# Keeping the retrieval dots' token rows in PSUM all the time, in a fused encoder layer on one core

## The reference

```python
# attention branch (8 heads, query/key width 96, value width 64), for each block of 128 queries
s = qn @ k_nope + qr @ k_rope
p = softmax(s); o = p @ v
# channel sublayer: retrieval over 16384 experts, 8 heads, top 16 each: 128 experts for every token
u = take(w_u, expert)                    # one row of 1024 values for each token and expert
h = einsum('cd,ced->ce', x, u)           # the "dots"
a = gelu(h) * gate
y = einsum('ce,ced->cd', a, take(w_v, expert))
```

## Time and profile before

| | |
|---|---|
| median of 3 runs | 3766.79 us (3752.15 to 3831.59) |
| the profiled execution | 3753.76 us, its span 3752.0 us |
| first dot, first slot of the loop of group 0 | 510 us, 688 us |
| DMA | 1225 MB, of which 1074 MB gathers |

### The profile page before, as it was taken

The page is one execution under the profiler, slowest core; times in us unless marked ns, Lnnn a source line. Parts: engine busy times, 40 slices in busy tenths (PEclk is TensorE's granted clock), DMA queues, the critical chain, the costliest instruction groups (busy, mean ns, idle before and its releaser), DMA issues.

```text
span 3752.0 us, 40793 instructions
## 1 busy us (share of the span) xinstructions
PE 2602.4 (69%) x13952; PEld 2128.5 (57%) x13952; DVE 2224.7 (59%) x5048; ACT 1618.5 (43%) x1846; POOL 2169.2 (58%) x2075
## 2 busy tenths in 40 slices
PE   6998966587886765777886666767976754544455
PEld 3456655465765664566765655657856644444444
DVE  5233166786655666776666666766566575565542
ACT  1121024455554444555554444555554444344344
POOL 3000035577687566677676556676775566666664
PEclk9999987787998886888998887888988876667667
DMA  4203469899999999999999999999999999999997
GB/s 173 93 29 105 146 257 344 298 352 346 400 409 407 359 362 346 345 349 375 409 409 383 356 346 337 347 342 386 409 409 366 347 341 352 354 337 351 339 351 294
DMA packets 341858, 1225.09 MB, mean 327 GB/s; under 512 B 37841, under 2 KB 45522, under 8 KB 341138
## 3 DMA queue, kind: packets, MB, share of 16 engines
q0 software_dynamic: 294912, 1073.87, 76.2%
q1 hardware_dynamic: 34226, 118.98, 8.5%
q10 hardware_dynamic: 12512, 29.63, 2.1%
HBM read 1206.61 MB, written 15.73 MB: 326 GB/s over the span
## 4 chain that ended last, share of the span: by engine, by line
PE 35%; another core or an unknown queue 21%; ACT 14%; issue 12%; POOL 7%; DMA 5%; DVE 4%; DVEq 1%; ACTq 0%; SPq 0%
PE acc L647 16%; ACT av L1174 10%; POOL rows L347 4%; POOL rows L338 4%; DMA rows<-in_peer_v,ids_peer 3%; PE fA L566 3%; PE mB L612 3%; PE fA L524 2%; PE fB L578 2%; PE mB L542 1%; PE mB L406 1%; DVE rows L946 1%; PE fB L376 1%; DMA rows<-in_peer_u,ids_peer 1%
## 5 line engine op out<-in xcount | busy, mean ns | idle before, releaser
L647 PE MATMUL acc<-ident,av 128*128 128x128 f32 x8192 | 1314.2, 320 | 1019.2 <-ACT av L1174 602.0
L647 PEld LDWEIGHTS acc<-ident,av 128*128 128x128 f32 x8192 | 1140.1, 167 | 1205.8 <-ACT av L1174 687.4
L1174 ACT ACTIVATE av<-rows,coef 128x1024 f32<-128x1024 f32 x1024 | 1155.9, 1145 | 1354.8 <-remote 709.5
L338 POOL DMA_INDIRECT rows<-in_peer_u,ids_peer x1024 | 1070.4, 1045 | 722.6 <-DVE ids_peer L926 309.4
L347 POOL DMA_INDIRECT rows<-in_peer_v,ids_peer x1024 | 1050.7, 1026 | 696.1 <-ACT av L1174 404.7
L946 DVE CUSTOM_DVE_ANT_0 rows<-rows,fB 128x1024 f32<-128x1024 f32 x538 | 647.8, 1216 | 360.6 <-DMA rows<-in_peer_u,ids_peer 322.9
L946 DVE CUSTOM_DVE_ANT_0 rows<-rows,hh 128x1024 f32<-128x1024 f32 x486 | 584.0, 1221 | 157.4 <-DMA rows<-in_peer_u,ids_peer 118.4
L612 PE MATMUL mB<-hT_g,wring 128*128 128x256 f32 x1024 | 246.5, 396 | 1.1 <-ACT hT_g L1136 1.1
L566 PE MATMUL fA<-hT_g,wring 128*128 128x256 f32 x1024 | 241.9, 391 | 3.6 <-issue 3.6
L612 PEld LDWEIGHTS mB<-hT_g,wring 128*128 128x128 f32 x1024 | 202.8, 204 | 28.6 <-ACT hT_g L1136 1.5
L566 PEld LDWEIGHTS fA<-hT_g,wring 128*128 128x128 f32 x1024 | 198.1, 198 | 33.9 <-issue 7.2
(11 more groups left out here) (170 smaller groups left out, 2233.1 us busy)
## 6 DMA issues: line engine op xcount, KB each, us to landing
wring<-in_wstream SPq DMA_DIRECT2D x192, 512.0 KB
rows<-in_peer_u,ids_peer POOLq DMA_INDIRECT x1024
rows<-in_peer_v,ids_peer POOLq DMA_INDIRECT x1024
hT_g<-in_x SPq DMA_DIRECT2D x8, 512.0 KB, 3.6
hres_spill<-KT ACTq DMA_DIRECT2D x8, 512.0 KB, 2.6
hT_spill<-rows ACTq DMA_DIRECT2D x1, 4096.0 KB
wring<-in_wstream SPq DMA_DIRECT2D x16, 256.0 KB
hh<-hres_spill ACTq DMA_DIRECT2D x4, 1024.0 KB
```

The lines of the kernel that those rows point to most:

```text
L338: pool.indirect_dma_start(u_rows[:, ring(g, i, NU), :], None, peer_u, bass.IndirectOffsetOnAxis(ap=ids_peer[:, t, s:s + 1], axis=0)).then_ ...
L647: last = mm(acc[:, tok(k)], av[:, i % NAV, tok(k)], ident[:, :], is_transpose=True, start=i % SLOTS == 0 and k % 4 == 0, stop=i % SLOTS == ...
L1174: s.activation(av[:, i % NAV, :], v_rows[:, ring(g, i, NV), :], ACT.Copy, scale=coef[:, b, i % BATCH:i % BATCH + 1]).then_inc(scaled, 1)
```

## The change

All dots read h1 from fB. For that, fB is freed of the front in every group after the first:

- In groups 1 to 3, the probabilities are turned in two halves through m1: four transposes (step a+7), a DVE copy of 512 columns (a+8), four transposes (a+9), a second copy (a+10). Group 0 still turns all eight through fB.
- The product with V of each head goes to 64 columns of m0 (`pv_at`), the bank that the queries use. So PE must wait with it until the queries of two heads later have been evicted, and with queries until the output of an earlier head has been read. Group 0 uses 64 columns of m1.
- DVE divides the output of each head by itself (a reciprocal of one column and a multiplication of 64 columns), where it did eight heads in one go.
- The turned output is copied in two halves.
- Gates, output projection and layer norm use m0 and m1 in the place of fB's halves (`front_banks`). PE's first such matmul waits until DVE has read the previous group's result out of mB (`y_read`), a wait that stood in front of the K stage before.
- Attention now ends at step 90, so M, O, L and K start ten steps later (M0 = 95, O0 = 143, L0 = 159, K0 = 171), with the lists moved accordingly, and LEAD goes from 40 to 32. Gates start after the last head's output is turned, where they started before it.

```diff
-LEAD = 40
+LEAD = 32
...
-M0, M_PERIOD = 85, 6
-O0 = 133
-L0 = 149
-K0, K_PERIOD = 161, 4
-
-PS0 = 162
+M0, M_PERIOD = 95, 6
+O0 = 143
+L0 = 159
+K0, K_PERIOD = 171, 4
...
+        front_banks = (fA[:, 0:512], fA[:, 512:1024], m0, m1)
+        q_ps_at, first_pv, pv_at = m0[:, 0:GROUP], m1[:, 0:VD], m0[:, GROUP:GROUP + VD]
...
+                        if g > 0 and h > 2:
+                            pe.wait_ge(o_done, g * TILES * H + h - 2)
...
+                            for k in range(TT // 2):
+                                last = tr(m1[:, tok(k)], probs[:, tok(k)])
+                            last.then_inc(probsT_ps, 1)
+                    if m == a + 9 and g > 0:
+                        pe.wait_ge(probsT_sb, 2 * n + 1)
+                        for k in range(TT // 2):
+                            last = tr(m1[:, tok(k)], probs[:, tok(k + TT // 2)])
+                        last.then_inc(probsT_ps, 1)
+                    if m == a + 12:
+                        pe.wait_ge(probsT_sb, 2 * n + 2)
+                        if positive(n):
+                            pe.wait_ge(o_done, n)
+                        if g > 0:
+                            pe.wait_ge(q_nope, g * H + min(u + 3, H))
+                            pe.wait_ge(q_rope, g * H + min(u + 3, H))
...
+                            if g > 0:
+                                pe.wait_ge(y_read, (g - 1) * TILES + 1)
...
+                            v.tensor_copy(probsT[:, 0:512], m1[:, :]).then_inc(probsT_sb, 1)
+                    if m == a + 10 and g > 0:
+                        dve.wait_ge(probsT_ps, 2 * n + 2)
+                        v.tensor_copy(probsT[:, 512:1024], m1[:, :]).then_inc(probsT_sb, 1)
+                    if m == a + 13:
+                        dve.wait_ge(pv_ps, n + 1)
...
+                        v.reciprocal(rrow[:, qt, h:h + 1], rowsum[:, qt, h:h + 1])
...
-            def dot(g, m, i):
-                in_ps = m >= PS0 or g + 1 == GROUPS
-                h1_copied = min(g + 2, GROUPS) * TILES
-                again = m == PS0 and g + 1 < GROUPS
+            def dot(g, i):
...
-                v.tensor_tensor_reduce(out=row, in0=row, in1=h1, scale=1.0, scalar=0.0, op0=ALU.mult,
+                v.tensor_tensor_reduce(out=row, in0=row, in1=fB[:, :], scale=1.0, scalar=0.0, op0=ALU.mult,
```

More of the change, by code:

```diff
@@ L511, in front @@
                             pe.drain().then_inc(w_free, 1)
-                    if m == a + 2:
+                    if m == a + 3:
                         if qt == 0:
@@ L536, in front @@
[L536 to L542, removed]
+                    n = g * TILES * H + u
+                    if m == a + 7:
+                        pe.wait_ge(probs_sb, n + 1)
+                        if positive(n):
+                            pe.wait_ge(probsT_sb, 2 * n)
+                        if g == 0:
+                            for k in range(TT):
+                                last = tr(fB[:, tok(k)], probs[:, tok(k)])
+                            last.then_inc(probsT_ps, 2)
+                        else:
+                            for k in range(TT // 2):
+                                last = tr(m1[:, tok(k)], probs[:, tok(k)])
+                            last.then_inc(probsT_ps, 1)
@@ L543, in front @@
                                       start=k == 0, stop=k == TT - 1)
                         last.then_inc(pv_ps, 1)
[L545 to L551, removed]
+                    for part in range(2):
+                        if h == H - 1 and m == a + 14 + part:
+                            pe.wait_ge(o_done, n + 1)
+                            if positive(2 * (g * TILES + qt) + part):
+                                pe.wait_ge(oT_sb, 2 * (g * TILES + qt) + part)
+                            for c in range(2):
+                                last = tr(m0[:, tok(c)], o_sb[:, tok(2 * part + c)])
+                            last.then_inc(oT_ps, 1)
@@ L588, in front @@
                             for half in range(2):
-                                last = mm(banks[2 * t + half], mT[:, k, tok(t)], w[:, half * 512:(half + 1) * 512],
+                                last = mm(front_banks[2 * t + half], mT[:, k, tok(t)], w[:, half * 512:(half + 1) * 512],
                                           start=k == 0, stop=k == KD - 1)
@@ L937, in dot @@
                 dve.wait_ge(u_in[ring(g, i, NU)], landed(g, i, NU))
-                if in_ps and (i % SLOTS == 0 or again):
-                    dve.wait_ge(h1T_sb, h1_copied)
+                if i % SLOTS == 0:
+                    if g == 0:
+                        dve.wait_ge(h1T_sb, TILES)
                     dve.drain()
@@ L972, in peer @@
                 if has_slot(g, m + LEAD + AHEAD, last):
-                    dot(g, m, m + LEAD + AHEAD)
+                    dot(g, m + LEAD + AHEAD)
                 if m % BATCH == 5 and has_slot(g, m + LEAD + BATCH, last):
@@ L997, in _ @@
                 if 0 <= m - US0 < LEAD + AHEAD:
-                    dot(-1, m, STEPS + m - US0)
+                    dot(0, m - US0)
                 for k in range(LEAD // BATCH + 1):
@@ L1121, in front @@
                         for j in range(2):
-                            last = s.activation(sg[:, j, :], banks[dc % 2][:, j * GROUP:(j + 1) * GROUP], ACT.Sigmoid,
+                            last = s.activation(sg[:, j, :], front_banks[dc % 2][:, j * GROUP:(j + 1) * GROUP], ACT.Sigmoid,
                                                 bias=bg[:, j, dc:dc + 1])
```

88 lines of the change are left out of this document (39 added, 49 removed).

## The result

The changed kernel takes 3826.24 us (median of 4 runs, 3819.98 to 3841.16), the kernel before 3763.24 us (4 runs). The ratio is 1.0163 with a 95% interval of 1.0132 to 1.0195: **1.6% slower**, where 0.8% was forecast. The profiled execution took 3827.17 us, its span is 73.4 us longer than that of before (3825.4 against 3752.0).

The account below looks back on a forecast made before the run. No engine was near full; the loop's pace was some 3 us per slot, DMA-limited in gates and output. 3753.8 + 19 (PSUM dots) + 4 (group 0's front) + 7 (seam) = 3784 us; range 3690 to 3875 us.

Parts of the forecast that it names:

- rival of late completions: Gates, output and attention: PE's results seen late under a faster POOL, 63 and 29 us more, 3857 us; chance 0.26.
- PSUM dots, 19 us lost: Steps 0 to 161 of three groups: slots go from 3.15 to 3.19 us, 19 us lost, between -20 and +49.
- The 3.25 us of the key stretches: Worst case for the dots changing sides: 0.10 us more per slot, 49 us lost.
- nothing that the dots read changes it: Gates and output projection: DMA engines are the limit at 406 GB/s, 207 us for 66 slots, whatever the dots read.
- Halves and handshakes, 0: Groups 1 to 3, per head: 22 us more DVE work and extra PE waits, hidden, charged 0.
- Group 0's front edge, 4 us: Group 0's unpaced front: turning the output now stands ahead of the gates, 4 us, between 0 and 6.
- The seam, 7 us: Between group 0's front and the loop: a second head's lists while POOL stands still, 7 us, between 0 and 7.
- The wait moved to the gates, 0: First output matmul waits for DVE's reading of mB: 0 to 4 us per group for three groups, taken as 0.
- POOL was the limit, 3700 us: Rival for the loop: POOL sets the pace in SBUF steps, freeing it gives 3700 us; chance 0.14.

Follow-up runs that it names:

- the kernel with SBUF dots: The changed kernel with the dots of steps 0 to 170 reading h1 from SBUF again: 3756.40 us, ratio 1.0049 to the kernel before; second time 3755.21 us, 1.0038.
- chip 7: One of the chips used: the kernel before takes 3463.29 us there; the changed kernel, otherwise unaltered, 3455.31 us, ratio 0.9978.
- the memset in the changed kernel: The changed kernel with one small POOL memset of 16 columns, and a wait for it, before each gather: 3758.02 us, ratio 1.0061 to the kernel before.

## Why the prediction was right, and where it was off

The forecast was 3784 us; 3826 us lies 42 us above it and 31 us below the rival of late completions, at 3857 us. So the direction was right, and half of the loss. The direction was read from a row (front steps with PSUM dots, 3.19 us) and not derived: the reason given, a freed POOL that runs ahead and waits, explains why nothing is gained, not why something is lost. That is partly luck.

- **PSUM dots, 19 us lost.** This is the term that was mis-sized. What it said of POOL came true: its issue fell from 1.13 to 0.95 us, and its waits grew by 1.5 times. But 0.08 us per slot for 513 slots is 41 us, and the experiment that takes back this alone gives some 40. I had taken the rate of all front steps with PSUM dots, 3.19 us. The 3.25 us of the key stretches, which I kept as the bound, was nearer: 3.23 and 3.19 us were measured.
- **Gates: "nothing that the dots read changes it".** Nearly so. Gates and output took 211 to 214 us where 207 stood, at 397 to 403 GB/s in place of 406. From dot to dot they went from 3.22 and 3.25 us to 3.32 and 3.31, and with SBUF dots they stand at 3.28 and 3.30. So most of this loss stays when the operand is taken back.
- **Late completions** stood as a rival at 3857 us. They are in the traces, and there are more of them after the change. Their price in the gates was too high: 211 to 214 us for 66 slots, where 228 were reckoned. From one dot's start to the next, attention (steps 0 to 84) went from 3.16 to 3.32 us, in the repeats from 3.12 to 3.26, where 3.25 was reckoned; the first 64 key steps went from 3.27 to 3.36 us, in the repeats from 3.25 to 3.32.
- **Halves and handshakes, 0.** Right: the halves alone cost nothing in the loops, and the copies wait under half a microsecond.
- **Group 0's front edge, 4 us.** The first dot starts at 510.60 us, at 510.42 before: 0, where the traces that keep this edge in either form lie between 506.7 and 513.5.
- **The seam, 7 us.** POOL's timeline at its end, to be held against the earlier trace rows:

```profile
656.88 0.94 POOL L347 DMA_INDIRECT rows<-in_peer_v,ids_peer  x1 [0.30 <-issue]
674.84 0.94 POOL L338 DMA_INDIRECT rows<-in_peer_u,ids_peer  x1 [17.01 <-DVE dots L963]
```

  17.0 us against 11.0, 6 us. Moving the lists brought 8.
- **The wait moved to the gates, 0.** Not separated by any run. It is within what the kernel with SBUF dots loses beside the seam, some 10 us, and gates and output, 0.05 us per slot slower in that kernel, are where these lie.
- **POOL was the limit, 3700 us.** False where it was to be forecast. On chip 7, where completions aren't late, a freer POOL goes with 0.2% less time; that is the direction of this rival, at a seventh of its size.

What stays open: the step from the PSUM operand to its 40 us. That the operand costs them is shown; that it does so through late completions is argued, and the memset in the changed kernel speaks against it ahead of the keys. DVE's reading of PSUM beside PE's writing was not tried apart. Open too is why completions of PE are seen late while POOL issues gathers back to back, and why not on chip 7. The runs show that it goes with the distance of the gathers and not with the bytes. Since only the traces of the late chips lack updates, the recording itself may have a part in the lateness; no run here tells.

## What to carry to other kernels

An engine that is not the limit may be too fast: where semaphore updates arrive in pairs and everything stands still until POOL stops, don't expect a gain from freeing POOL, and try a small brake on it. Hold a mechanism against its count by stage, not over the whole trace: the totals of pairs and times looked ordered here, and the stages show that the pairs fell where the time did not. When an edit moves a kernel between two mixtures of stages that the trace already shows, take the rate of the stage whose load is most like the new one, not the mean. Read the trace of group 0 apart from the loops: what costs nothing under the slots' cover cost 17 us there.

## What the runs showed of the hardware

- Same kernel, two kinds of chip: the kernel before takes 3463.29 us on one, 3732.14 to 3763.24 us on the others; the changed kernel's last group runs at 2.57 against 3.05 us per slot.
- A gather issue takes POOL 0.95 us and 0.30 us more to the next, with 4 KB rows or 2 KB rows. DVE dots with both operands in SBUF raise it to 1.13 us. The Trainium skill ("SBUF — State Buffer", section Who interferes with whom) infers that making descriptors isn't stalled by such an instruction. The runs show that the issue of a gather is slowed: the kernel that differs in the operand alone has a mean of 1.04 us against 0.95 over all its gathers. A gather also reads its row numbers from SBUF (`ids_peer`), and no run tells whether that read waits or the making of descriptors.
- A memset of 0.13 us with its wait adds 0.10 us to the distance of two gathers, two of them 0.60 us.
- Close pairs of PE's completions, by the usual distance of two gathers: 122 to 127 at about 1.25 us throughout, 91 to 100 where SBUF dots widen it in part of the time, 38 and 60 at 1.34 us; on chip 7 none at 1.24 us.
